# The chunked recurrence of an RWKV block: head products paired across the halves of TensorE, growth and outputs in one PSUM bank, the last growth left out

## The chip, the cores and the metric

One Trainium2 chip, one of its NeuronCores. The metric is the device time of one execution in microseconds (us), lower is better. PE is TensorE, DVE is VectorE, ACT is ScalarE, POOL is GpSimd.

## What is computed

The kernel runs two transformer blocks one after the other over 16 meta tokens and 512 real tokens of width 1024: gated feed-forward layers, a mixer with stick-breaking attention and an RWKV-7 recurrence (first block), three attention branches (second block), and norms. The change touches the RWKV-7 recurrence of the first block alone. For each of 8 heads of width 64, with a state S of 64 x 64:

```python
def step(S, inp):
    r_t, w_t, k_t, v_t, kk_t, a_t = inp
    sa = jnp.einsum('bhij,bhj->bhi', S, -kk_t)
    S = (S * w_t[:, :, None, :] + sa[..., None] * (kk_t * a_t)[:, :, None, :]
         + v_t[..., None] * k_t[:, :, None, :])
    return S, jnp.einsum('bhij,bhj->bhi', S, r_t)
```

The outputs of the 512 real tokens go through a norm over each head, a bonus term and a gate, and then into the output projection.

## The kernel before

The recurrence is computed in nine chunks of 64 tokens (CH); the first holds the meta tokens. Within a chunk the 64 steps become matrix products: scores between the prepared keys and queries, the inverse of a triangular matrix built by doubling, a solve against the incoming state, the growth of the state, and the outputs. Two heads share the 128 partitions: four pairs p, and in each pair one head on partitions 0 to 63 and one on 64 to 127. `heads_in_turn` (L2185) lists for each head its own half `f` and the opposite half `u`. Each product of a head is a 64x64 by 64x64 float32 matmul, which TensorE takes as two records in the profile, on one quadrant of its array: input rows `f` or `u`, output partitions `f` or `u`. A group of eight such products goes to one PSUM bank and is then copied or masked out by one instruction of ACT or DVE.

A chunk c goes through 16 steps k:

- k = 0 (L2209): two scores groups, "nb" and "xc", each 64x128 a head, input and output on half f. DVE masks each (L2368).
- k = 1: the first factors "tus" (L2221), one group onto f and then one onto u; for chunk 0 some identity products (L2231); then three turns (L2240), each of four transposes, of BETA, CHI and VV, whose results ACT copies in halves into BCV (L2338, L2340).
- k = 2: the product of scores and values, "xv" (L2249), onto u; ACT copies it into VH (L2345).
- k = 3, 5, 7, 9, 11: a "half" (L2259), input f, onto u, of TU with a level mask LT that POOL makes (L2420); ACT copies it into PM (L2349).
- k = 4, 6, 8, 10, 12: a "corner" (L2269 onto f, L2271 onto u, head by head in turn); DVE adds it to TU (L2388). The last corner has the u part alone (L2390).
- k = 12, for chunks 2 to 5: a product of the bonus (L2278), one 128x512 matmul; DVE multiplies it (L2396).
- k = 13: "ks", keys by the state (L2285), onto u; DVE adds VH into RS (L2401).
- k = 14: "solve" (L2294), input u, onto f; ACT copies it into SA (L2353).
- k = 15: "update", the growth of the state, in two groups (L2301, L2305) that accumulate in one bank; DVE adds the state (L2404) and scales it to the next one (L2407). For c > 0 the outputs in three groups (L2315) that accumulate in another bank; ACT copies them into Y_R (L2357).

`mixed_order` (L2143) sets the order on every engine: in round r the chunks c with 0 <= r - 4c < 16 take their step k = r - 4c, the oldest chunk first. So up to four chunks are under way, four rounds after one another, and from round 12 to 35 every round holds three or four steps of different chunks. Each step's groups are issued whole, one group after another. What is called a round of four in the tables below is four values of r, from the scores of one chunk to those of the next.

PSUM banks are handed out by `taken_in_turn` (L324): the i-th group of the list `chunk_takes` gets bank i mod 4 (banks 0 to 3) and waits for the release of the group four places before it. Groups that use two banks (first factors and corners) take pairs 4/5 and 6/7 in turn, so that each waits for the release of the one two places before. The engines meet through semaphores only; the order in each engine is the order written out.

After the recurrence the head norm starts on PE when the eighth output copy ("yb") is there and the ninth state ("state"); ACT and DVE also wait for that state. No weight is loaded by the recurrence; the loads for the output projection are issued by SyncE well before.

## Time and profile before

| what | us |
| --- | --- |
| median of 3 runs | 2481.23 |
| lowest and highest | 2478.31, 2481.26 |
| the profiled execution | 2476.59 |
| its span | 2474.6 |
| mean granted TensorE clock | 0.989 |

The time of an execution is a little longer than its span, the stretch that the profiler covers. All rows below are of the profiled execution, and their times count from the start of its span. A row of the windows view has the stretch, its length, the busy time and number of records of PE, PEld (weight loads), DVE, ACT and POOL, then the granted TensorE clock, the DMA engines' busy share and GB/s. In a row of the timeline "x16" is the number of records merged into it, and what stands in brackets is how long the engine had been idle before it and which work ended that. Busy times of PE take in a matmul's latency, so a matmul's 218 ns is longer than the distance to the next one.

### The profile page before, as it was taken

How to read it: one execution, taken by the hardware profiler on the slowest of the kernel's cores; microseconds unless marked ns; L12 is line 12 of the kernel's file. 1: busy time of each engine (PE TensorE's matmuls, PEld its weight loads, DVE VectorE, ACT ScalarE, POOL GpSimd, SP SyncE). 2: the span in 40 equal slices, each digit the busy share in tenths (PEclk: the TensorE clock that was granted, in tenths of full speed). 3: DMA queues.
4: the chain of work that ended last, by engine and by line, in shares of the span. 5: the costliest groups of instructions: out<-in, count | busy, mean ns of one | idle time of the engine just before them, and what ended most of it. 6: DMA issues, size and time to landing. Idle time of an engine off the chain costs nothing.

```text
span 2474.6 us, 48942 instructions
## 1 busy us (share of the span) xinstructions
PE 2421.6 (98%) x20393; PEld 2228.6 (90%) x20393; DVE 1707.5 (69%) x2951; ACT 1080.8 (44%) x1980; POOL 98.3 (4%) x108
## 2 busy tenths in 40 slices
PE   9999999999999999999999999999989999999998
PEld 7999999996887989898999999898877888989896
DVE  6878775646556979688879585243986445879694
ACT  5444343334434535356535243212874224535252
POOL 0000001000320000001000002000000000000001
PEclk9999999999999999999999999999999999999999
DMA  4233232220001332332232233222112333233332
GB/s 152 84 106 103 101 96 90 80 81 12 4 10 46 104 110 96 111 96 77 83 122 94 97 102 97 71 93 85 52 51 77 98 94 102 95 103 103 103 93 70
DMA packets 72378, 213.00 MB, mean 86 GB/s; under 512 B 12796, under 2 KB 20028, under 8 KB 72032
## 3 DMA queue, kind: packets, MB, share of 16 engines
q1 hardware_dynamic: 70496, 209.03, 26.4%
q8 instruction: 162, 2.65, 0.4%
q0 software_dynamic: 480, 0.73, 0.1%
q14 instruction: 56, 0.46, 0.1%
q10 hardware_dynamic: 1184, 0.12, 0.0%
HBM read 207.61 MB, written 2.20 MB: 85 GB/s over the span
## 4 chain that ended last, share of the span: by engine, by line
PE 84%; DVE 8%; ACT 5%; issue 3%; DMA 0%; DVEq 0%; ACTq 0%
PE PS L866 21%; PE PS L1401 20%; PE PS L1358 11%; PE PS L1360 10%; PE PS L1359 10%; DVE WL L951 2%; ACT WH L939 1%; PE PS L2259 1%; PE PS L1709 1%; PE PS L1708 1%; PE PS L1710 1%; DVE P L2913 1%; ACT P L2879 1%; PE PS L1236 1%; PE PS L2209 1%
## 5 line engine op out<-in xcount | busy, mean ns | idle before, releaser
L1358 PE MATMUL PS<-OPH,WH 128*128 128x256 f32 (+1 forms) x2112 | 603.0, 285 | 7.4 <-ACT TMP L1456 2.7
L1360 PE MATMUL PS<-OPH,WL 128*128 128x256 f32 (+1 forms) x2112 | 600.0, 284 | 0.0
L1359 PE MATMUL PS<-OPL,WH 128*128 128x256 f32 (+1 forms) x2112 | 598.1, 283 | 0.0
L939 ACT ACTIVATE WH<-WR 128x1024 fp32r<-128x1024 f32 (+2 forms) x277 | 275.6, 995 | 564.3 <-PE PS L866 272.9
L951 DVE TENSOR_TENSOR WL<-WR,WH 128x1024 fp32r<-128x1024 f32 (+2 forms) x277 | 318.5, 1150 | 190.5 <-ACT WH L939 190.2
L1358 PEld LDWEIGHTS PS<-OPH,WH 128*128 128x128 f32 x2112 | 401.4, 190 | 11.2 <-DVE OPL L1108 3.2
L1359 PEld LDWEIGHTS PS<-OPL,WH 128*128 128x128 f32 x2112 | 401.2, 190 | 1.1 <-issue 0.7
L1360 PEld LDWEIGHTS PS<-OPH,WL 128*128 128x128 f32 x2112 | 400.5, 190 | 0.0
L939 ACT ACTIVATE WH<-SUMS 128x512 fp32r<-128x512 f32 x352 | 211.0, 623 | 231.3 <-DVE SUMS L977 188.8
L951 DVE TENSOR_TENSOR WL<-SUMS,WH 128x512 fp32r<-128x512 f32 x352 | 234.1, 684 | 21.0 <-ACT WH L939 20.5
L866 PE MATMUL PS<-NHI,WH 128*128 128x264 f32 (+2 forms) x976 | 237.9, 309 | 1.0 <-ACT TMP L2633 1.0
L866 PE MATMUL PS<-NLO,WH 128*128 128x264 f32 (+2 forms) x976 | 236.0, 308 | 0.0
L866 PE MATMUL PS<-NHI,WL 128*128 128x264 f32 (+2 forms) x976 | 235.3, 306 | 0.0
L866 PEld LDWEIGHTS PS<-NHI,WH 128*128 128x128 f32 x976 | 157.5, 189 | 12.7 <-issue 1.6
L866 PEld LDWEIGHTS PS<-NLO,WH 128*128 128x128 f32 x976 | 158.6, 189 | 8.8
L866 PEld LDWEIGHTS PS<-NHI,WL 128*128 128x128 f32 x976 | 157.9, 189 | 8.3
L1401 PE MATMUL PS<-HH_A,WH 128*128 128x264 f32 (+1 forms) x572 | 152.4, 321 | 0.0
L1401 PE MATMUL PS<-HL_A,WH 128*128 128x264 f32 (+1 forms) x572 | 152.4, 321 | 0.0
L1401 PE MATMUL PS<-HH_A,WL 128*128 128x264 f32 (+1 forms) x572 | 152.0, 320 | 0.0
L1533 DVE TENSOR_TENSOR T<-PS,RT 128x528 f32<-128x528 f32 (+1 forms) x64 | 44.7, 699 | 148.1 <-PE PS L1401 148.1
L1401 PE MATMUL PS<-HH_B,WH 128*128 128x264 f32 (+1 forms) x476 | 127.1, 321 | 0.0
L1401 PE MATMUL PS<-HL_B,WH 128*128 128x264 f32 (+1 forms) x476 | 126.4, 321 | 0.0
(475 smaller groups left out, 4610.9 us busy)
## 6 DMA issues: line engine op xcount, KB each, us to landing
WR<-in_ffn_up SPq DMA_DIRECT2D x64, 512.0 KB, 3.9
WR<-in_ffn_down SPq DMA_DIRECT2D x64, 512.0 KB, 3.7
WR<-in_ffn_gate SPq DMA_DIRECT2D x56, 512.0 KB, 3.9
WR_MORE<-in_ffn_gate SPq DMA_DIRECT2D x32, 512.0 KB, 4.5
WR_MORE<-in_ffn_up SPq DMA_DIRECT2D x24, 512.0 KB, 4.1
WR<-in_ffn_down SPq DMA_DIRECT2D x32, 384.0 KB, 3.2
WR<-in_w_gate SPq DMA_DIRECT2D x24, 512.0 KB, 3.6
WR<-in_w_out SPq DMA_DIRECT2D x16, 512.0 KB, 3.6
```

The source lines that it names most:

```text
L866: last = e.matmul(bank, left[:, cols], right[:, a:b] if right.shape[1] == L else right, start=(kt == 0 and left is wh and right is hi), st ...
L939: e.activation(split_unit(i)[0][:, 0:w], src, ACT.Copy).then_inc(S["w_hi"], 1)
L951: e.tensor_tensor(lo[:, 0:w], src, hi[:, 0:w].bitcast(F32), ALU.subtract).then_inc(S["w_lo"], 1)
L1236: last = e.matmul(at[:, i:i + 1], data[:, a:a + 128], cst("ones", 128, 1), start=opens, stop=k == DT - 1, skip_group_check=True)
L1358: e.matmul(o, wh[:, at:at + 128], hi, start=k == 0 and s in (1, 2, 5), stop=False, skip_group_check=True)
L1359: e.matmul(o, wh[:, at:at + 128], lo, start=False, stop=False, skip_group_check=True)
L1360: last = e.matmul(o, wl[:, at:at + 128], hi, start=False, stop=k == 3, skip_group_check=True)
L1401: last = e.matmul(bank, left[:, cols], right[:, a:b], start=t == first and left is wh and right is hi, stop=t == end - 1 and left is wl, s ...
L1533: e.tensor_tensor(tcols(t, R), pcols(pair_of["down", f, c, m][0], R), tcols(RT, R), ALU.mult).then_inc(S["d_t"], 1)
L1708: e.matmul(o, NHI[:, kt, a:a + 128], wh[:, c], start=kt == 0, stop=False)
L1709: e.matmul(o, NHI[:, kt, a:a + 128], wl[:, c], start=False, stop=False)
L1710: last = e.matmul(o, NLO[:, kt, a:a + 128], wh[:, c], start=False, stop=kt == DT - 1)
```

## The change

The order of PE in the recurrence is no longer one step after another. The rounds are of four kinds, r mod 4: `with_scores`, `with_state`, `with_solve`, `with_growth`. In each, pairs of groups that use different quadrants are issued head by head in turn:

- the first scores (step 0) of one chunk with the values product of the chunk before, which moves from step 2 to step 4;
- keys by state (step 13) with the first part of the growth (moved from step 15 to 13); halves of steps 9 and 5 with the first two parts of the outputs (moved from step 15 to 13); the two groups of the first factors with each other;
- the solve (step 14) with the second scores, which move from step 0 to step 2;
- the half of step 11 with the second part of the growth, and the half of step 7 with the last part of the outputs (step 15).

The three turns of a chunk are spread over the steps 1 (VV), 2 (BETA) and 3 (CHI). The bonus product moves from step 12 to 11. Growth and outputs share bank 3 for good; all other single groups now take banks 0 to 2 in turn. DVE's growth addition waits for the outputs, and ACT's output copy waits for that addition. The growth of chunk 8, whose state nobody reads, is left out, and the head norm waits for state 8. On ACT and DVE the order within a round stays the oldest chunk first.

The diff, cut to its core:

```diff
+        TURNED_AT = {1: 2, 2: 0, 3: 1}
+        GROWTH_BANK = 3
...
-        chunk_bank = taken_in_turn(chunk_takes, 4)
+        chunk_bank = taken_in_turn(chunk_takes, 3)
...
+            def with_scores(steps):
+                if 12 in steps:
+                    corner(steps[12], 4)
+                if 8 in steps:
+                    corner(steps[8], 2)
+                if 4 in steps:
+                    corner(steps[4], 0)
+                new, old = steps.get(0), steps.get(4)
+                if new is not None:
+                    bank = taken("nb", new)
+                if old is not None:
+                    q.wait_ge("xc", old + 1)
+                    q.wait_ge(*turned_out(old, 2))
+                    values_bank = taken("xv", old)
+                for p, f, u in heads_in_turn:
+                    if new is not None:
+                        scored = scores_product(new, bank, BETA, p, f)
+                    if old is not None:
+                        seen = e.matmul(PS[u, values_bank, 64 * p:64 * p + 64], chunk_homes[old % 4][1][f, p, 0],
+                                        chunk_turned[old % 5][f, 2, p], start=p == 0, stop=True, skip_group_check=True)
...
+            def with_state(steps):
+                late = steps.get(13)
+                if late is not None:
+                    q.wait_ge("state", late)
+                    bank = taken("ks", late)
+                    q.wait_ge("grown", min(late, 1))
+                    q.wait_ge("yb", max(late - 1, 0))
+                    for p, f, u in heads_in_turn:
+                        kept = e.matmul(PS[u, bank, 64 * p:64 * p + 64], KAPPA[f, p, tokens_of(late)],
+                                        ST[f, late % 2, p], start=p == 0, stop=True, skip_group_check=True)
+                        if late < 8:
+                            growth_product(late, 0, p, f)
+                    kept.then_inc(S["ks"], 1)
+                for k, x in (9, 0), (5, 1):
+                    c = steps.get(k)
+                    if c is not None:
+                        bank = half_ready(c, (k - 3) // 2)
+                    for p, f, u in heads_in_turn:
+                        if c is not None:
+                            halved = half_product(c, bank, p, f, u)
+                        if late:
+                            outs_product(late, x, p, f)
+                    if c is not None:
+                        halved.then_inc(S["half"], 1)
...
+            def with_solve(steps):
+                late, new = steps.get(14), steps.get(2)
+                if late is not None:
+                    q.wait_ge("rs", late + 1)
+                    q.wait_ge("tu", tu_at[late, 5])
+                    solve_bank = taken("solve", late)
+                if new is not None:
+                    bank = taken("xc", new)
+                for p, f, u in heads_in_turn:
+                    if late is not None:
+                        solved = e.matmul(PS[f, solve_bank, 64 * p:64 * p + 64], chunk_homes[late % 4][2][u, 1, p],
+                                          RS[u, p], start=p == 0, stop=True, skip_group_check=True)
+                    if new is not None:
+                        scored = scores_product(new, bank, CHI, p, f)
...
+                if 10 in steps:
+                    corner(steps[10], 3)
+                if 6 in steps:
+                    corner(steps[6], 1)
+                if new is not None:
+                    turn(new, 0)
+
+            def with_growth(steps):
+                late = steps.get(15)
+                if late is not None:
+                    q.wait_ge("sa", late + 1)
+                c = steps.get(11)
+                if c is not None:
+                    bank = half_ready(c, 4)
+                for p, f, u in heads_in_turn:
+                    if c is not None:
+                        halved = half_product(c, bank, p, f, u)
+                    if late is not None and late < 8:
+                        grown = growth_product(late, 1, p, f)
...
+                for p, f, u in heads_in_turn:
+                    if c is not None:
+                        halved = half_product(c, bank, p, f, u)
+                    if late:
+                        seen = outs_product(late, 2, p, f)
...
+                    halved.then_inc(S["half"], 1)
+                    turn(c, 1)
...
+            for r in range(4 * 8 + 16):
+                steps = {k: (r - k) // 4 for k in range(r % 4, 16, 4) if 0 <= r - k < 36}
+                (with_scores, with_state, with_solve, with_growth)[r % 4](steps)
...
                     q.wait_ge("outs", c)
-                    e.activation(Y_R[:, :, t0:t0 + CH], four(chunk_bank["outs", c][0]), ACT.Copy).then_inc(S["yb"], 1)
+                    q.wait_ge("grown", min(c + 1, 8))
+                    e.activation(Y_R[:, :, t0:t0 + CH], PS[:, GROWTH_BANK, 256:512].rearrange("p (a n) -> p a n", a=4),
+                                 ACT.Copy).then_inc(S["yb"], 1)
...
-                if k == 15:
+                if k == 15 and c < 8:
                     q.wait_ge("updated", c + 1)
-                    e.tensor_tensor(STT, four(chunk_bank["update", c][0]), ST[:, c % 2], ALU.add).then_inc(S["grown"], 1)
+                    q.wait_ge("outs", c)
+                    e.tensor_tensor(STT, four(GROWTH_BANK), ST[:, c % 2], ALU.add).then_inc(S["grown"], 1)
...
             q.wait_ge("yb", 8)
-            q.wait_ge("state", 9)
+            q.wait_ge("state", 8)
```

## Rows read from the trace of the kernel before

**Rows 1.** The page: each engine's busy time.

```profile
PE 2421.6 (98%) x20393; PEld 2228.6 (90%) x20393; DVE 1707.5 (69%) x2951; ACT 1080.8 (44%) x1980; POOL 98.3 (4%) x108
```

**Rows 2.** The windows view of the recurrence, one row from scores to scores.

```profile
613.98:623.31 9.33, 7.24 (x170) 6.80 (x170) 3.46 (x5) 3.90 (x10) 1.45 (x2) 1.00 0.01 2
623.31:631.69 8.38, 7.38 (x241) 6.87 (x238) 4.72 (x7) 3.80 (x10) 2.87 (x4) 1.00 0.02 4
631.69:641.35 9.66, 8.99 (x321) 8.51 (x318) 6.05 (x10) 4.56 (x12) 4.18 (x6) 1.00 0.02 3
641.35:652.21 10.86, 10.65 (x384) 10.14 (x382) 7.48 (x12) 4.95 (x13) 3.64 (x5) 1.00 0.02 5
652.21:665.32 13.11, 13.05 (x435) 11.77 (x432) 8.15 (x14) 5.25 (x14) 4.36 (x5) 1.00 0.02 5
...
691.30:704.25 12.95, 12.89 (x435) 11.69 (x432) 8.36 (x15) 5.24 (x14) 4.37 (x5) 1.00 0.02 4
704.25:737.71 33.46, 29.13 (x1021) 27.18 (x1016) 15.06 (x29) 8.60 (x24) 7.09 (x9) 1.00 0.02 4
```

**Rows 3.** Timeline of PE: start, length, line, operands, records; chunk 0, then chunk 8.

```profile
615.77 0.75 PE L2221 MATMUL PS<-CHANNELS 64*64 64x64 f32 x26
...
616.83 0.63 PE L2231 MATMUL PS<-CST,CHI 64*64 64x64 f32 x8
617.29 0.63 PE L2231 MATMUL PS<-CST,CHANNELS 64*64 64x64 f32 x8
...
727.09 0.68 PE L2259 MATMUL PS<-TU,SMALL 64*64 64x64 f32 x16 [0.53 <-issue]
...
728.24 0.27 PE L2269 MATMUL PS<-SMALL,TU 64*64 64x64 f32 x1
...
728.72 0.22 PE L2271 MATMUL PS<-TU,SMALL 64*64 64x64 f32 x1
```

**Rows 4.** Timeline of PE: the bonus product, its multiplication (DVE), transposes.

```profile
702.04 1.12 PE L2278 MATMUL PS<-BONUS,CST 128*128 128x512 f32 x2
703.09 0.27 PE L2269 MATMUL PS<-TMP,TU 64*64 64x64 f32 x1
...
703.20 0.69 DVE L2396 TENSOR_TENSOR BONUS<-CHANNELS,PS 128x512 f32<-128x512 f32 x1 [0.62 <-PE PS L2278]
...
707.55 0.62 PE L2240 MATMUL PS<-CST,CHANNELS 128*64 128x128 f32 x4
...
708.98 0.39 PE L2294 MATMUL PS<-TMP,TU 64*64 64x64 f32 x6
```

**Rows 5.** Timeline of ACT and DVE: copies and additions behind groups of PE.

```profile
700.63 0.38 ACT L2357 ACTIVATE Y_R<-PS 128x256 f32<-128x256 f32 x1 [1.78 <-PE PS L2315]
700.93 0.38 ACT L2349 ACTIVATE SMALL<-PS 128x256 f32<-128x256 f32 x1
...
703.86 1.28 DVE L2388 TENSOR_TENSOR TU<-TU,PS 128x512 f32<-128x512 f32 x2
...
727.80 0.38 ACT L2349 ACTIVATE SMALL<-PS 128x256 f32<-128x256 f32 x1 [2.64 <-PE PS L2259]
...
729.00 0.69 DVE L2388 TENSOR_TENSOR TU<-TU,PS 128x512 f32<-128x512 f32 x1 [1.69 <-PE PS L2271]
730.30 0.42 DVE L2404 TENSOR_TENSOR STT<-PS,ST 128x256 f32<-128x256 f32 x1 [0.61 <-PE PS L2305]
```

**Rows 6.** Timeline of PE: the first values product.

```profile
620.99 0.68 PE L2249 MATMUL PS<-BCV,XC 64*64 64x64 f32 x16 [1.61 <-ACT BCV L2340]
```

**Rows 7.** Timeline of PE and ACT: the end of the recurrence.

```profile
732.44 0.51 PE L2271 MATMUL PS<-TU,SMALL 64*64 64x64 f32 x10 [0.48 <-ACT SMALL L2349]
...
734.71 0.38 ACT L2353 ACTIVATE TMP<-PS 128x256 f32<-128x256 f32 x1 [2.32 <-PE PS L2294]
737.28 0.38 ACT L2357 ACTIVATE Y_R<-PS 128x256 f32<-128x256 f32 x1 [2.18 <-PE PS L2315]
```

**Rows 8.** The chain of waits, 714 to 722 us: start, length, what.

```profile
720.35 0.83 issue
```

More of the change, by code:

```diff
@@ new lines, in tokens_of, with taken, half_ready, half_product @@
+            def tokens_of(c):
+                return slice(CH * c, CH * c + CH)
+            def taken(*name):
+                bank, free = chunk_bank[name]
+                q.wait_ge(*free)
+                return bank
+            def half_ready(c, x):
+                q.wait_ge("lt", pm_at[c, x])
+                q.wait_ge("tu", tu_at[c, x])
+                return taken("half", c, x)
+            def half_product(c, bank, p, f, u):
+                TU, LT = chunk_homes[c % 4][2:4]
+                return e.matmul(PS[u, bank, 64 * p:64 * p + 64], LT[f, p], TU[f, 0, p], start=p == 0, stop=True,
+                                skip_group_check=True)
@@ new lines, in turn @@
+            def turn(c, g):
+                bank = taken("tr", c, g)
+                width = 2 * CH if c < 8 else CH
+                for p in range(4):
+                    last = e.transpose(PS[0:width, bank, 128 * p:128 * p + 128],
+                                       (BETA, CHI, VV)[g][:, p, CH * c:CH * c + width], cst("ident"))
+                last.then_inc(S["turned"], 1)
+            def with_scores(steps):
[19 more added lines that the diff above has]
+                if new is not None:
+                    scored.then_inc(S["scored"], 1)
+                if old is not None:
+                    seen.then_inc(S["xv"], 1)
@@ L2252, in pe_rwkv @@
-                if 3 <= k < 13 and k % 2 == 1:
-                    x = (k - 3) // 2
-                    bank, free = chunk_bank["half", c, x]
-                    q.wait_ge("lt", pm_at[c, x])
-                    q.wait_ge("tu", tu_at[c, x])
-                    q.wait_ge(*free)
-                    for p, f, u in heads_in_turn:
-                        last = e.matmul(PS[u, bank, 64 * p:64 * p + 64], LT[f, p], TU[f, 0, p], start=p == 0,
-                                        stop=True, skip_group_check=True)
-                    last.then_inc(S["half"], 1)
@@ L2288, in pe_rwkv @@
-                if k == 14:
-                    bank, free = chunk_bank["solve", c]
-                    q.wait_ge("rs", c + 1)
-                    q.wait_ge("tu", tu_at[c, 5])
-                    q.wait_ge(*free)
-                    for p, f, u in heads_in_turn:
-                        last = e.matmul(PS[f, bank, 64 * p:64 * p + 64], TU[u, 1, p], RS[u, p], start=p == 0,
-                                        stop=True, skip_group_check=True)
-                    last.then_inc(S["solved"], 1)
@@ L2494, in dve_head_norm @@
             q.wait_ge("outs", 8)
[L2495 removed]
+            q.wait_ge("state", 8)
             for k in range(4):
```

259 lines of the change are left out of this document (120 added, 139 removed).

## The prediction, made before the changed kernel ran

> **What bounds the kernel now.** I read the page first: TensorE (PE) is busy for 2421.6 us, 98% of the span [rows 1], so only a change that shortens PE's own order, or a wait in it, can pay. Then the windows view, cut where the scores of a new chunk begin. The recurrence is the stretch from 613.98 to 737.71 us, 123.7 us of 2474.6. Its nine pieces [rows 2] show three regimes. In the first two PE is busy 7.24 of 9.33 us and 7.38 of 8.38: waits count. From the fourth to the eighth PE is covered (12.89 of 12.95 us in the last full round, four rounds nearly alike): work counts. In the last, 33.46 us, it is 29.13 busy, and waits count again. VectorE (DVE) has 8.36 us of work in a full round and ScalarE (ACT) 5.24. The granted clock is 1.00 in every piece, also where PE is least busy, so I give the clock no share.
>
> The timeline then gives PE's prices. A half, a group of eight head products (16 matmul records) on two quadrants, starts at 727.09 and its copy at 727.80, 0.71 us later. A corner of 32 records, which uses both output halves, has its first at 728.24 and its last at 728.72, and its addition starts at 729.00, 0.76 us after its start [rows 3, 5]: twice the records in the same time, some 0.47 us and the latency. So a quadrant, not the issue of instructions, sets the pace, and two groups can share 0.47 us if they lie on different quadrants; this is what the change tries. A scores group takes 0.9 us (two before 615.77, from 613.98); the identity products on one quadrant take 0.46 us for eight records [rows 3]. Twelve transposes take 1.43 us (707.55 to 708.98), 0.48 for four; alone between small tiles, with an entry and an exit of their own each time, I take 0.6 as an estimate [rows 4]. The bonus product costs 1.05 us (702.04 to 703.09) [rows 4].
>
> Other prices [rows 5]: a wide DVE operation takes 0.69, one behind another 0.60 (1.28 for two); a narrow one 0.42; ACT's copy 0.38, but 0.30 from start to start when both are ready (700.63, 700.93), 0.40 for the turned copies. PE follows a finished copy by 0.05 us.
>
> **The parts, and their sum.** PE's work in a full round after the change: three corners 1.41, scores with values in their shadow 0.9; kept/growth, two halves with outputs, first factors, each 0.47 = 1.88, a turn 0.6; solve under the second scores 0.9, two corners 0.94, a turn 0.6; three halves (two carry growth and outputs) 1.41, a turn 0.6, the bonus 1.05. Together 10.3 us, against 12.95 now [rows 2]. Were this all, a full round would win 2.65 us. It isn't: each group now sits between buffers that are released later. With three banks in turn instead of four, I wrote out which release each group waits for. Let u be the start of the half of step 7, which now carries the last outputs.
>
> - Turn of step 3 waits for the copy of half 11. ACT has the output copy ahead of it, which now waits for the outputs (u + 0.71), for the growth addition that itself waits for the outputs (0.42 and 0.04), then 0.30, 0.38 and 0.05: u + 1.9. PE is done at u + 0.94. Wait 0.95.
> - The youngest corner waits for the addition of the oldest one (its pair of banks), which sits behind the bonus multiplication on DVE: the bonus starts 1.16 us after its product (702.04 to 703.20), takes 0.60, the addition 0.42; PE could go 0.25 earlier. Wait 0.25.
> - Half 9 takes the bank of the new scores. DVE masks them after three corner additions and the product's end: u + 6.4 to u + 7.1, PE is there at u + 6.6. Wait 0.5.
> - Half 7 takes the bank of the second scores, whose mask is behind two corner additions on DVE (u + 10.8, 11.4, mask 12.0 to 12.7); PE is there at u + 12.05. Wait 0.65.
>
> Sum of waits 2.35, a round of 12.65, say 12.7. The last three full rounds of before (665.32 to 704.25) are 13.0 each on average [rows 2], so 0.3 each, 0.9; the one before them (13.11) wins 0.4.
>
> First four rounds: now 9.33 + 8.38 + 9.66 + 10.86 = 38.2 [rows 2]. What goes there is the wait of the values product for the turned copies (1.61 us for the first chunk, [rows 6]), as it moves from step 2 to step 4. Round one after: scores 0.9, identity 1.4, first factors 0.47, turn 0.6, scores 0.9, turn 0.6, half 0.47, turn 0.6, 0.45 left of waiting for its copy behind the turned copies, corner 0.47: 6.9. Round two by the same list: 6.9 of work and 0.7 of waits, 7.6. Round three 8.75 and 1.5 (scores' bank, second mask), 10.25; round four 9.25 and 1.5, 10.75. Sum 35.5, so 2.7 less. Note that the third round gets longer than now.
>
> Tail: today the last outputs follow the last solve by growth (0.47 behind ACT's copy) and three output groups, 734.71 to 737.28 [rows 7], 2.57 us. After, two output groups are already done and growth is left out: 0.38 + 0.05 + 0.71 = 1.15, so 1.4 less. In the three rounds before, half 11 no longer waits behind five groups of growth and outputs, but its copy waits for the output copy: half 729.7, outputs 730.2, growth addition 730.9, output copy 731.35, its copy 731.65, corner 732.1 instead of 732.44 [rows 7]: 0.35 each, 1.0. Together 2.4. The last growth's two DVE operations (0.42 each) stand beside output products, hidden by them: nothing. The tail also holds a stall of 0.83 us with no releaser [rows 8]; I count it neither as gone nor as new.
>
> Sum: 2.7 + 0.4 + 0.9 + 2.4 = 6.4, less 0.4 for more such stalls where dense pairs follow each other (bounds: none, and one of 0.83 us in each of the nine rounds, 7 us; I stay near none, since the corners already run at that density and PE is covered for 12.89 of 12.95 us in the full round that holds them [rows 2]). 6.0 us. The profiled execution took 2476.6 us (span 2474.6), so 2470.6 on its scale; it lies 4.6 under the median of the three runs, 2481.2, to which I apply the difference: 2475.2. What follows is PE-bound too (98%) and its weights are loaded already (DMA share 0.02 here), so it should shift whole.
>
> What is costed at nothing: the five level masks on GpSimd (4.37 us a round, [rows 2]) are released by the half before and needed two steps later, some 5 us, so they stay under PE's work; were that cover gone, each half would wait 0.8 us. The sums of scores and values (ACT) move from step 2 to step 4, needed at step 13. The bonus product moves one step ahead, the same work. The second mask moves from step 0 to step 2 and is the fourth wait above. No DMA is issued by the moved steps, and no queue of one is passed. The wait for a ninth state falls away; the head norm waits for the last output copy as now.
>
> The unshown price is that of the pairs: no row has a group of halves with outputs, or a solve beside scores. Lower bound 0.47, that of a corner (same alternation of output halves over one input half); upper bound 0.94, the two in turn. I take 0.47, since the halves and outputs have exactly the corner's pattern.
>
> The Trainium skill, page "TensorEngine Tiling (Array Packing)", section "PSUM Bottleneck", speaks against such a change: tiling makes TensorE quicker, not the copying out of PSUM. By engine totals it would not bind here (DVE 8.4 under PE's 10.3), and a round would be 10.3; by my waits for single copies it is 12.7. No run here shows which yet.
>
> **Rivals.**
> *The copies keep up* (0.06). DVE's total is 8.36, ACT's 5.24 a round; if their queues fit better than I wrote out, the full rounds fall to 10.3 to 11: four times 2.3 more, and some in the fill, 2464. Against: the four waits above follow from queue order.
> *New waits take nearly all* (0.32). Each wait 0.1 to 0.2 us longer than walked, and a full round is 13.0 or over; rounds three and four give back what one and two win. The tail's 2.4 and part of the fill stay: 2478 (-1 to -5).
> *Pairs run one behind the other* (0.12, slower). Alternating onto the other half could stall each product on its neighbour. Six pairs lie on the round's chain (half 7, half 9, half 5, first factors, values, solve), 0.47 each, 2.8 a round: 15.5 for 13.0 in four rounds, +10, while fill and tail keep some 4: 2487. It decides from 0.64 us a pair on (6.0 us over 36 pairs on the chain). Against it stands the corner row. That the kernel's pairs are no pairs at all is in this case.
>
> **How the numbers follow.** My case, 0.50: 5 to 9 us faster, 2472 to 2476. A measurement of this kernel tells 0.2%, 5 us, from no change, and my centre lies just beyond. Faster is 0.50 + 0.06 = 0.56, same 0.32, slower 0.12. Range: down to 2469 for waits that are shorter, up to 2482.5 through the second case and the beginning of the third; runs of one kernel differ by 3 us.
>
> **What would show it.** Windows: nb-to-nb distance about 7, 7.6, 10.3, 10.8, then 12.7 four times, a tail near 31; PE busy under 12 in a full round. Waits: the step 3 turn and half 9 on ACT and DVE, the half of step 7 on the second mask. 32 records of a half/output pair within 0.5 us. Last scores to first centering 31 us instead of 33.5. I am wrong if pairs take 0.9, if full rounds are 11 or less, or if new stalls appear at another place than these four.

## The result, and the profile after

| | before | after |
| --- | --- | --- |
| median, runs side by side (7 and 7) | 2480.28 us | 2488.15 us |
| lowest and highest | 2476.90, 2482.19 | 2485.33, 2491.07 |
| the profiled execution | 2476.59 | 2485.33 |
| its span | 2474.6 | 2483.3 |
| recurrence, first scores to head norm | 123.73 | 132.18 |

The ratio is 1.0034, with a 95% interval from 1.0024 to 1.0043: slower by 7.9 us. The forecast was 6 us faster, 2475.2, with a range up to 2482.5. The recurrence alone took 8.45 us more, so that is where to look; on the page the kernels are otherwise alike:

```profile
PE 2416.2 (97%) x20361; PEld 2216.7 (89%) x20361; DVE 1708.1 (69%) x2949; ACT 1080.1 (43%) x1980; POOL 95.4 (4%) x108
...
q8 instruction: 162, 2.65, 0.4%
```

PE has 5.4 us less busy time than in [rows 1] and 32 of its records fewer (the last growth), and yet the time is longer: what grew is idle time. The last line, a DMA queue that carries instructions (packets, MB, share), will matter below; before has the same one.

The windows view of after, cut at the scores of each chunk as in [rows 2] (stretch, length, busy time and records of PE, PEld, DVE, ACT, POOL, clock, DMA share, GB/s):

```profile
614.51:622.65 8.14, 6.86 (x151) 5.98 (x153) 3.46 (x5) 3.52 (x9) 1.45 (x2) 1.00 0.01 2
622.65:631.48 8.83, 7.91 (x251) 6.75 (x245) 5.04 (x7) 3.80 (x10) 2.90 (x4) 1.00 0.01 4
631.48:642.62 11.14, 9.73 (x329) 8.54 (x324) 6.07 (x9) 4.46 (x12) 3.64 (x5) 1.00 0.01 3
642.62:654.39 11.77, 10.80 (x390) 9.57 (x390) 7.26 (x12) 4.95 (x13) 3.77 (x5) 1.00 0.02 5
654.39:668.85 14.46, 11.72 (x443) 9.76 (x440) 8.52 (x14) 5.13 (x14) 3.63 (x5) 1.00 0.02 5
...
697.48:712.16 14.68, 11.76 (x443) 9.79 (x438) 8.55 (x15) 5.12 (x14) 3.63 (x5) 1.00 0.02 4
712.16:746.69 34.53, 24.97 (x1017) 22.26 (x1007) 14.21 (x27) 8.58 (x25) 7.00 (x9) 0.95 0.02 4
```

Only the first round is shorter, 8.14 for 9.33. A full round takes 14.4 us where before took 13.0 and I had walked 12.7, though PE's busy time fell from 12.9 to 11.8 as meant. Grouped in three, against before and against the walk:

| stretch | before | walked | after |
| --- | --- | --- | --- |
| first four rounds | 38.23 | 35.5 | 39.88 |
| four full rounds | 52.04 | 50.8 | 57.77 |
| the rest | 33.46 | 31.1 | 34.53 |

Next, whether the pairs run as pairs. PE's timeline of after, where the half of step 5 (L2224) runs with the second part of the outputs (L2242), and then the first factors begin (L2333):

```profile
700.67 0.24 PE L2224 MATMUL PS<-TU,TMP 64*64 64x64 f32 x1
700.68 0.27 PE L2242 MATMUL PS<-XC,BCV 64*64 64x64 f32 x1
...
701.16 0.22 PE L2333 MATMUL PS<-CHANNELS 64*64 64x64 f32 x1
```

16 products in 0.48 us, where eight took 0.47 in [rows 3]. The unshown price was right, at its lower bound. The same timeline, those rows of the full round from 692.14 to 706.80 that had an idle stretch before them:

```profile
694.22 0.66 PE L2261 MATMUL PS<-CST,CHI 128*128 128x128 f32 x4 [0.92 <-ACT SMALL L2440]
...
699.44 0.24 PE L2224 MATMUL PS<-TU,SMALL 64*64 64x64 f32 x1 [0.45 <-DVE NB L2461]
...
700.55 0.27 PE L2242 MATMUL PS<-CHANNELS,ST 64*64 64x64 f32 x1 [0.42 <-issue]
...
704.37 0.27 PE L2253 MATMUL PS<-TU,SMALL 64*64 64x64 f32 x1 [0.56 <-issue]
...
706.80 0.24 PE L2224 MATMUL PS<-TU,TMP 64*64 64x64 f32 x1 [0.41 <-DVE XC L2461]
```

Three of the waits that I had written out stand at their places: the turn of step 3 behind ACT's copy, half 9 behind the mask of the new scores, half 7 behind the second mask. The fourth, 0.25 us at the youngest corner, is there too: 0.37 us pass between the last product before it (696.59) and its first (696.96). Its idle time is just too short for a row here; one round later it has one:

```profile
724.84 0.24 PE L2251 MATMUL PS<-SMALL,TU 64*64 64x64 f32 x1 [0.15 <-DVE TU L2483]
```

Between the waits are two stops that nothing released. From start to start they are longer than the idle time in brackets, which counts from the modelled end of the product before: 0.64 us (699.91 to 700.55) and 0.78 (703.58 to 704.37), 1.42 us in this round. The first falls into the middle of a group: 15 of the 16 records of that part of the outputs had gone, and the last came 0.64 us late. No semaphore stands there.

The waits view of PE over the recurrence (line, what it waited for, us, times, longest), after:

```profile
PE PS L2224 <- DVE NB L2461: 3.3, 7, 0.7
PE PS L2261 <- ACT TMP L2440: 2.8, 3, 0.9
PE PS L2224 <- DVE XC L2461: 2.2, 6, 0.5
PE PS L2251 <- ACT SMALL L2440: 1.9, 2, 1.3
PE PS L2261 <- ACT SMALL L2440: 1.8, 2, 0.9
PE PS L2242 <- issue: 1.8, 4, 0.8
PE PS L2253 <- ACT SMALL L2440: 1.6, 1, 1.6
```

All its rows on copies and masks sum to 18.0 us in 29 waits, and those on "issue" to 6.0 us in 12. The same view of before has 4.9 in 7 and 2.2 in 4. From start to start, the four full rounds of after hold seven stops without a releaser, 4.84 us in all, and 10.84 us in 16 waits at the four places; those of before hold no such stop that the view lists.

### The profile page after: what moved, and what is told of

It reads as the page before. It is cut to its first block, busy times and chain, and to the rows that moved or that the text cites. A ratio compares the mean times of both kernels' runs of the same rounds, so it can differ in the third digit from the quotient of the medians.

```text
span 2483.3 us, 48900 instructions
## 1 busy us (share of the span) xinstructions
PE 2416.2 (97%) x20361; PEld 2216.7 (89%) x20361; DVE 1708.1 (69%) x2949; ACT 1080.1 (43%) x1980; POOL 95.4 (4%) x108
## 4 chain that ended last, share of the span: by engine, by line
PE 83%; DVE 8%; ACT 5%; issue 3%; DMA 1%; DVEq 0%; ACTq 0%
PE PS L866 21%; PE PS L1401 20%; PE PS L1358 11%; PE PS L1359 10%; PE PS L1360 10%; DVE WL L951 2%; ACT WH L939 1%; PE PS L1709 1%; PE PS L1708 1%; PE PS L1710 1%; DVE P L3007 1%; ACT P L2973 1%; PE PS L1236 1%; DVE SUMS L977 1%; PE PS L2228 1%
## 5 line engine op out<-in xcount | busy, mean ns | idle before, releaser
L1358 PEld LDWEIGHTS PS<-OPH,WH 128*128 128x128 f32 x2112 | 402.3, 190 | 10.3 <-DVE OPL L1108 2.9
L866 PEld LDWEIGHTS PS<-NHI,WH 128*128 128x128 f32 x976 | 157.3, 189 | 12.7 <-issue 1.6
```

The source lines that it names most:

```text
L866: last = e.matmul(bank, left[:, cols], right[:, a:b] if right.shape[1] == L else right, start=(kt == 0 and left is wh and right is hi), st ...
L1358: e.matmul(o, wh[:, at:at + 128], hi, start=k == 0 and s in (1, 2, 5), stop=False, skip_group_check=True)
```

## The experiments

Two theories. **S, supply:** the stops without a releaser are PE out of instructions. I counted PE's records (loads, products, semaphores) in the two traces: 14 of the 16 stops in the two recurrences stand 256 records apart (give or take one), or a multiple of 256, and each of these ends 2.2 to 3.0 us after a 16 KB packet of the instruction queue has started, at whatever product it then is. The two others (627.76 in after, 727.09 in before) are off this count and stay unexplained. **Q, quadrants and copies:** PE is paced by its quadrants and by the copies and masks alone, and the stops are a few odd delays. A third, **W**, adds to either that the waits that I walked are worth their price.

**1. A dense stretch by itself.** The kernel before with a block of products between recurrence and head norm: 512 products of 64x64 by 64x64 in the order of a corner, then 128 with 256 columns. Nothing waits in it.

```diff
+            for n in range(32):
+                tok = slice(CH * (n % 8), CH * (n % 8) + CH)
+                for p, f, u in heads_in_turn:
+                    e.matmul(PS[f, 4, 64 * p:64 * p + 64], KAPPA[f, p, tok], BETA[f, p, tok], ...)
+                    e.matmul(PS[u, 5, 64 * p:64 * p + 64], BETA[f, p, tok], KAPPA[f, p, tok], ...)
```

> The kernel before, with products between the recurrence and the head norm that nothing reads and nothing holds up: 512 products of 64x64 by 64x64 (2048 records: a weight load and a matmul, twice, for each), in the corner's pattern on four quadrants, then 128 products of 64x64 by 64x256 (512 records). Theory S (PE's instructions come in blocks of 256, and a block takes some 3.5 us however fast the records run): the 2048 records take 8 x 3.5 = 28 us instead of 8 x 1.9 = 15 us, in bursts with a gap at every 256th record; the 512 wide ones take about 14 us, set by the quadrants, without gaps. Rival Q (the quadrants alone set the pace, the gaps of the changed kernel are waits for data that the profile does not name): 15 us and no gaps, 14 us. The whole kernel is 43 or 29 us longer than the one before.

Measured: 2523.24 us in one run, 42.7 over before. Its timeline of PE with the idle stretches, the windows from stop to stop and then of the part with 256 columns, its waits view and the line of the instruction queue:

```profile
750.87 0.21 PE L2448 MATMUL PS<-CHANNELS 64*64 64x64 f32 x1 [1.38 <-issue]
...
754.34 0.21 PE L2448 MATMUL PS<-CHANNELS 64*64 64x64 f32 x1 [1.38 <-issue]
```

```profile
743.65:747.39 3.74, 2.09 (x128) 1.96 (x128) 2.92 (x6) 0.00 (x0) 0.00 (x0) 1.00 0.36 131
...
750.87:754.34 3.47, 2.09 (x130) 1.96 (x129) 0.00 (x0) 0.00 (x0) 0.00 (x0) 1.00 0.02 5
743.65:765.50 21.85, 12.55 (x768) 11.75 (x768) 2.92 (x6) 0.00 (x0) 0.00 (x0) 1.00 0.08 26
...
767.60:783.00 15.40, 15.01 (x255) 12.63 (x246) 0.00 (x0) 0.00 (x0) 0.00 (x0) 1.00 0.01 2
```

```profile
PE PS L2448 <- issue: 11.0, 7, 1.7
```

```profile
q8 instruction: 172, 2.82, 0.5%
```

128 products and 128 loads, 256 records, run in some 1.9 us, then PE stands still until 3.47 to 3.75 us have passed since the last stop ended. Six such blocks, up to the end of the seventh stop at 765.57, take 21.92 us, 3.65 each, or 14.3 ns a record. Seven stops sum to 11.0 us. With 256 columns a product is longer, and PE is busy for 15.01 of 15.40 us. 2560 records more have brought ten packets and 0.17 MB more: 256 records to a packet of 16 KB. Instructions come in such packets while the kernel runs, and in this stretch no block came in less than 3.47 us. S is shown for this stretch and Q, which had 29 us more for the whole kernel, is out.

The trace also shows the rhythm. Each of the packets starts 1.06 to 1.53 us after PE has gone on from the stop before, and PE goes on again 2.2 to 2.7 us after the packet's start. So a block costs a little over 1 us until the next packet starts, and the packet's 2.2 us or more. In the recurrences of all 14 traces the latter holds without exception: PE never enters a block less than 2.16 us after its packet has started.

The Trainium skill, page "Perfetto Trace Analysis", section "The 4-stage abstract model", gives an instruction 64 bytes; 256 of them are 16,384 bytes, one such packet. Its page "Trainium Architecture — The Big Picture", section "The software stack", says that a program's instruction streams are brought to the engines when it is loaded; the 162 packets within one execution speak against reading this as "all of them", and the measurement decides.

**2. Moving the count.** The kernel after, with small products in place of some filler of an earlier stage, to shift all later products by a part of a block. A miss of design: the filler that I changed is called in the first feed-forward too.

```diff
-            for _ in range(times):
+            for _ in range(times - 2):
...
+            for _ in range(34):
+                e.matmul(PS[:, 3, 0:8], FILLER[:, 0:128], FILLER[:, 0:8], start=True, stop=True, skip_group_check=True)
```

> The changed kernel, with two of the 14 opening filler products replaced by 34 narrow ones: some 128 records more ahead of the recurrence, no other work. Theory S: the gaps without a releaser (699.91 and 703.58 in the profile of the changed kernel, each 256 records apart or a multiple of it) sit at other groups, again at multiples of 256 records from one another, shifted by about 128 records; the time stays within 3 us. Rival Q (they are waits for data): the gaps stay at the same groups, the half of step 5 and the corner of step 10.

Measured: 2565.84 us in one run. The shift was of 780 records, three blocks and 12. In the trace 11 of the 12 stops of the recurrence stood again on the same count, so 12 records earlier in their groups. The twelfth, which was off the count in after (627.76), moved with its own product, by 12 records. A small step, not the one meant, but it goes as S said: the stops keep to the count and not to a product. The time says nothing; the products cost what they cost in the feed-forward.

**3. The two orders that my walk named.** The kernel after; in each round ACT takes the output copy behind the copies of the halves, and DVE the second mask ahead of the corner additions. Then each alone.

```diff
+        act_order = sorted(mixed_order, key=lambda ck: (4 * ck[0] + ck[1], ck[1] == 15))
-            for c, k in mixed_order:
+            for c, k in act_order:
...
+        dve_order = sorted(mixed_order, key=lambda ck: (4 * ck[0] + ck[1], ck[1] != 2))
-            for c, k in mixed_order:
+            for c, k in dve_order:
```

> The changed kernel with two queues put in another order, nothing else: ACT makes the output copy (step 15) last in its round, after the copies of the halves, and DVE makes the second mask (step 2) ahead of the corner additions. Theory W (the new waits for released banks make the round long): the waits of the step 3 turn (1.14 us) and of the half of step 7 (0.5 us) go, 1.5 us a full round, 5 full rounds and as many shorter ones: 10 us less than the changed kernel, 2478, under the kernel before. Theory S: the round cannot fall under 3.4 x 3.5 = 12 us whatever the waits, since it has some 900 records; freed stretches run into the next block: 0.5 us a round, 3 to 5 us less, 2484.

> The kernel after with one edit: in each round ScalarE takes the output copy behind the copies of the halves. It takes the first of my four waits away (0.95 us a full round, walked), over some seven rounds. W (my walk, each wait is worth what it is priced at): 4 to 6 us less than after, 2483. S with slack (a wait and a missing block of instructions can overlap): 2 to 4, 2485. If the two order edits together gave 8.3 and do not overlap, this and the next kernel sum to 8.3.

> The kernel after with the other edit: VectorE takes the second mask first in its round, ahead of the corner additions. It takes the fourth wait away (0.65 us a full round, walked). W: 3 to 4 us less than after, 2484.5. S with slack: 1 to 3, 2486.

Measured: both 2479.89 us, ratio to before 1.0002 (0.9992 to 1.0011), 8.3 less than after. The output copy alone 2481.03, 7.1 less; the mask alone 2484.58, 3.6 less. W's figures, 4 to 6 and 3 to 4, were low for the copy and right for the mask, and together they overlap by 2.4; for both at once W had 10. S's, 3 to 5 for both and 2 to 4 and 1 to 3 alone, were all too low: they let a wait and a stop overlap. The three stretches, of the kernel with both, then with the copy alone, in the windows view:

```profile
614.42:654.23 39.81, 35.30 (x1083) 30.67 (x1085) 22.15 (x33) 16.62 (x44) 11.65 (x16) 1.00 0.02 3
654.23:706.50 52.27, 46.40 (x1730) 38.90 (x1729) 33.63 (x56) 20.74 (x56) 15.51 (x20) 1.00 0.02 5
706.50:737.63 31.13, 24.43 (x1016) 21.46 (x1007) 13.94 (x27) 9.00 (x25) 7.00 (x9) 1.00 0.02 4
```

```profile
656.72:709.25 52.53, 46.76 (x1733) 39.10 (x1730) 34.02 (x56) 20.94 (x56) 15.04 (x20) 1.00 0.02 5
709.25:739.86 30.61, 24.26 (x1017) 21.44 (x1008) 13.94 (x27) 9.03 (x25) 7.03 (x9) 1.00 0.02 5
```

Look at the second stretch. Two waits a full round, 1.6 us as walked, are gone, and the four full rounds fall from 57.77 to 52.27: to just what before has, 52.04, and not to the 44.4 that my walk would give without them (four times 12.7 less 1.6). PE still idles 5.9 of these 52.27 us, a part of it before half 9. The stops without a releaser are untouched: seven, 4.66 us from start to start, where after has seven and 4.84. So the waits came off in full, and the stops stayed. The records that I counted in the stretch are 3476, 13.6 blocks, at 3.85 us each. Before's are 3468 in 52.04 us, 3.84 each, some 5% above the probe's 3.65. That the two meet doesn't show one cause: before has no listed stop in its full rounds, and a group alone takes 14.7 ns a record on its quadrants anyway.

**4. Cheaper order in the kernel before.** The two groups of the first factors, one after the other before, are issued as a pair.

```diff
-                    for w in range(2):
-                        for p, f, u in heads_in_turn:
+                    for p, f, u in heads_in_turn:
+                        for w in range(2):
```

> The kernel before with one pair of the change alone: the two groups of the first factors are issued head by head in turn, onto both output halves, without any new wait. PE's work falls by 0.47 us in each of nine chunks, in rounds where PE is covered. Theory W: 4 us less than before, a little under for the first two rounds. Theory S: a full round of before (13.0 us for some 890 records) already lies at 3.7 us for 256 records, so little of it shows: under 1.5 us less.

Measured: 2479.91 us, ratio 0.9995 (0.9986 to 1.0004), not to be told from no change. Full rounds, windows view:

```profile
652.32:704.72 52.40, 51.92 (x1732) 46.76 (x1725) 33.07 (x56) 21.07 (x56) 17.44 (x20) 1.00 0.02 5
```

52.40 for 52.04. But the run doesn't part the theories, since the pair was hardly worth anything: in full rounds the first factors take 0.78 us (0.96 in the first) from their first product to the first transpose, and 0.91 (1.07) before, so 0.11 to 0.13 a round and not 0.47. In before's order the first of the two groups already runs beside the end of the half ahead of it, on other quadrants. The half microsecond won in four rounds went into stops: one of 0.45 us from start to start at 675.31 and one of 0.22, both on the count of 256, where before ran through.

**5. More records, hardly more work.** The kernel before with 16 tiny products (8 columns) a chunk, 64 records, behind the first factors.

```diff
+                    for p, f, u in heads_in_turn:
+                        for w, o in enumerate((f, u)):
+                            last = e.matmul(PS[o, bank + w, 256:264], KAPPA[f, p, tok], BETA[f, p, CH * c:CH * c + 8],
+                                            start=False, stop=True, skip_group_check=True)
```

> The kernel before with 16 products of 64x64 by 64x8 more in step 1 of each chunk, on four quadrants, into unread columns of the first factors' banks: 64 records a chunk, hardly any columns. Theory S (a block of 256 PE instructions takes 3.5 us or more to arrive): 64 records cost 0.9 us in each of the rounds where PE is covered, 5 to 8 us in all, as if they were full products. Rival Q (the quadrants alone set the pace): 32 matmul records on four quadrants at some 25 ns each, 0.2 us a chunk, 2 us in all.

Measured: 2484.44 us, ratio 1.0021 (1.0011 to 1.0031), 4.6 over its own runs of before (2479.88). Nearer to S than to Q, and just under S's band. In the trace the four full rounds took 54.35 us, 2.3 more, for 256 records more: 3.74 us a block, the nearest to the probe's pace of all complete kernels. But it isn't stops that grew: the full rounds list only one, 0.44 us from start to start. The first factors with the tiny products take 1.33 us in most rounds, for 0.91, so the products' own time, 0.42 us a round and twice what Q had, is 1.7 of the 2.3. And the first four rounds grew too, by 1.8. This run speaks for a Q with a dearer product rather than for S.

**6. Fewer records, the same order.** The kernel after without two of the three parts of the outputs for chunks 1 to 7; then the same on the kernel with both orders. These parts lie on the quadrants opposite to the halves of steps 9 and 5 and run in their shadow (the pair above took 0.48 us).

```diff
-                        if late:
+                        if late == 8:
                             outs_product(late, x, p, f)
```

> The kernel after without the first two parts of the outputs (the state and the value part) for chunks 1 to 7: 16 products, 64 records of PE, fewer a chunk; every wait, bank and release stays. Left out of the computation: those two parts, so Y_R of these chunks is incomplete. The 16 products lie on quadrants opposite to those of the halves of steps 9 and 5, one for one. Theory S (PE's instructions arrive in blocks of 256 records, at least 3.5 us apart): 448 records fewer at 8.7 ns (what the padded kernel showed, 5 us for 576) to 14.5 ns (3.7 us over 256) each, 3.9 to 6.5 us less than after, about 2483.5, and fewer stalls without a releaser. Rival Q (quadrants and copies alone set the pace): the products are in the shadow of the halves, 0 to 0.5 us less, 2488. A fall of 2 or less speaks for Q.

> The kernel with both order edits, and without the two output parts of chunks 1 to 7 (64 records a chunk fewer; Y_R of these chunks is incomplete). With two waits gone it should hang on the supply more than after does. S: 4 to 6.5 us less than the kernel with both order edits, 2474 to 2476, faster than before though before does more of these products. Q: 0 to 0.5 less, 2479.5.

Measured: 2480.47 us, 7.7 less than after; and 2472.93, ratio 0.9968 (0.9955 to 0.9981), 7.0 less than with both orders. Q had 0 to 0.5. Windows of the first, and the half of step 9 that has lost its partner:

```profile
618.29:658.13 39.84, 35.52 (x1082) 30.86 (x1084) 21.50 (x33) 16.77 (x44) 12.21 (x16) 1.00 0.01 3
658.13:712.11 53.98, 45.28 (x1602) 38.25 (x1601) 33.51 (x56) 20.53 (x56) 15.84 (x20) 1.00 0.02 4
712.11:743.67 31.56, 23.20 (x921) 20.57 (x911) 14.31 (x27) 8.59 (x25) 6.98 (x9) 1.00 0.02 4
```

```profile
700.95 0.68 PE L2224 MATMUL PS<-TU,SMALL 64*64 64x64 f32 x16 [0.44 <-DVE NB L2461]
701.44 0.49 PE L2224 MATMUL PS<-TU,TMP 64*64 64x64 f32 x10
```

And the one stop without a releaser that the waits view of its four full rounds still lists:

```profile
PE PS L2253 <- issue: 1.1, 1, 1.1
```

The half alone takes 0.49 us from start to the next, as with a partner: on the quadrants the partner had been free. The first four rounds, from which no product was taken, are as in after (39.84 for 39.88). The four full rounds lost 3.8 us with 256 records, 14.8 ns a record, close to the probe's 14.3; over the recurrence the waits on copies hardly changed (17.3 us in 29), those on "issue" fell from 6.0 to 3.0. In the four full rounds the stops fell from 4.84 us in seven to 1.34 in one, from start to start: 3.5 of the 3.8 us. This is the run that shows the supply at work inside the recurrence. Both medians fell by more than S had said. Not all of it is supply: the last stretch fell by 3.0, of which up to 1.7 is a stretch of low clock that after's trace has there and this one hasn't (see below). In the trace of the second, full rounds fell by 2.4 (52.27 to 49.84) and the whole recurrence by 2.5 of the 7.0, under S's 4 and over Q's 0.5; the rest lies outside it, where the same instructions ran somewhat quicker, and I did not find why.

**7. Three parts without pairs.** On the kernel before: the values product at step 4; the end shortened (last growth out, last outputs' first two parts behind the keys by state); and both, with each round's outputs and their copy at its end.

```diff
-                if k == 2:
+                if k == 4:
                     bank, free = chunk_bank["xv", c]
```

```diff
+                    if c == 8:
+                        outs_products(c, (0, 1))
...
-                if k == 15:
+                if k == 15 and c < 8:
...
+                if k == 15 and c > 0:
+                    q.wait_ge("sa", c + 1)
+                    outs_products(c, (0, 1, 2) if c < 8 else (2,)).then_inc(S["outs"], 1)
```

> The kernel before with the values product and its copy moved from step 2 to step 4, unpaired, four banks as before. The prediction priced the waits for turned copies in the first four rounds; no new wait for a released bank is made here. If that term was right: the first two rounds fall by 1.6 and 1.2 us, the third by 0.7, and the whole by 2 to 3 us. If the copies that ACT makes are late for the next group instead (the turned copies stand ahead of the half's copy), less than 1 us is left.

> The kernel before with the end of the change alone: the growth of chunk 8 left out and its first two output groups issued at step 13; one output group follows the last solve. The prediction priced this at 1.4 us (copy of the solve to the last output copy 1.15 us for 2.57 us). Theory S adds nothing here, PE waits for data there: 1.4 us less, under what the runs can tell, to be read in the trace. Rival: the two output groups delay the last solve by their 0.94 us and half of it is given back.

> The kernel before with values at step 4, the short end, and the outputs of every chunk issued at the end of their round, behind the halves, as ACT's output copy is; nothing is paired and four banks are kept. Theory S: in full rounds nothing is gained (some 890 records a round, 13.0 us), in the fill 2 us, at the end 1.4 us and in the three rounds of the tail, where half 11 no longer waits behind three output groups, up to 1 us each: 5 us less than before, 2475. Theory W (new waits for released banks decide): the order of takes is new here too, so some full rounds grow, and 2478 to 2481.

Measured: values at step 4 2479.96 us, ratio 1.0001 (0.9991 to 1.0011); short end 2478.82, 0.9993 (0.9984 to 1.0003), the two not to be told from no change; all three 2477.27, 0.9987 (0.9978 to 0.9996), some 3 us less than before, between S's 2475 and W's 2478 to 2481, and the fastest complete kernel of the study. Windows of the first (first four rounds), of the second (its second round and the last stretch), and of the third:

```profile
618.23:657.09 38.86, 34.10 (x1094) 31.91 (x1094) 21.39 (x34) 16.83 (x44) 12.13 (x16) 1.00 0.01 4
```

```profile
624.18:634.21 10.03, 9.03 (x249) 8.52 (x242) 4.56 (x7) 3.80 (x10) 2.70 (x4) 0.83 0.02 3
...
708.18:739.43 31.25, 27.85 (x1000) 26.18 (x992) 14.38 (x27) 8.60 (x24) 7.09 (x9) 1.00 0.02 4
```

```profile
618.40:656.07 37.67, 33.77 (x1093) 31.71 (x1093) 21.27 (x34) 16.87 (x44) 12.68 (x16) 1.00 0.02 4
656.07:708.94 52.87, 52.24 (x1727) 47.29 (x1725) 33.76 (x56) 21.39 (x56) 17.00 (x20) 1.00 0.02 4
708.94:740.00 31.06, 27.60 (x1003) 26.07 (x998) 14.24 (x27) 9.26 (x25) 7.10 (x9) 1.00 0.02 4
```

The move of the values product wins a microsecond in the first round (its wait of [rows 6] is gone) and gives it back in the third and fourth, where the trace has two stops on the count of 256 (1.42 and 0.38 us from start to start), so the first four rounds stand at 38.86 for 38.23: the gain of 2.7 us that I had put on this stretch isn't in the move itself. The short end wins 2.2 us in the last stretch of its trace, where 1.4 was walked for it; its median moved by 1.1, within the noise. And no complete kernel got its four full rounds below 52 us.

## Why the prediction was wrong

**The price of a pair: right.** 0.48 us for 16 products.

**PE's work in a full round, 10.3 us: nearly right, but not all that bounds.** Without stops and waits, 42.1 of the 57.77 us are left, 10.5 a round. I read 12.89 busy of 12.95 us [rows 2] as PE's quadrants at work, and for before that stands: its blocks take from 2.90 to 5.02 us there, and at their ends no gap from start to start is over 0.16 us. What I didn't see is how near the supply lay: 3.84 us a block on average, against 3.65 in the probe where nothing else bound. A full round has some 869 records, 3.4 blocks, 12.4 us at the probe's pace (an estimate), whatever lies in whose shadow. Pairing halves the time of a group and leaves its instructions. A group alone is 32 records in 0.47 us, 14.7 ns each, which happens to be the pace of supply; a pair is 64 in 0.48, twice that pace. "So a quadrant, not the issue of instructions, sets the pace" was read from a single corner, and holds for one.

**The step that failed** is the last term of the sum, 0.4 us "for more such stalls where dense pairs follow each other", with "bounds: none, and one of 0.83 us in each of the nine rounds, 7 us; I stay near none, since the corners already run at that density". The corners do, but for half a microsecond at a time, with slower groups between them. The walked round of 12.7 holds 2.35 us of waits and then 869 records in the other 10.3, 11.9 ns each, quicker than they come. Over the recurrence the stops without a releaser rose from 3.10 us in four to 8.75 in twelve, start to start, so 5.65 more for the 0.4: nearer to the bound of 7 than to none. In the four full rounds, where before lists none, the walk missed by 7.0 us: 4.8 are these stops, 1.4 longer waits, 0.9 work. Waits and supply add up instead of hiding each other: taking two of the waits out left the stops as they were (run 3), and taking 256 records out of these rounds took 3.5 us of stops away (run 6). The step is the largest, not the only one: from 6.0 us less to 8.45 more are 14.4 us, of which the full rounds are 7.0 and the first four and the last stretch, below, 4.4 and 3.4 (less the 0.4).

**The four waits: right in place and nearly in price.** From start to start they took 1.14, 0.37, 0.66 and on average 0.55 us a full round, 2.7 together, the products' usual distance of some 0.05 each included; I had 0.95, 0.25, 0.5 and 0.65, together 2.35. Without the two that an order can remove, the median falls by 8.3 us, of which the output copy's is 7.1. In the full rounds I had 1.6 us for these two, and 1.4 were won (57.77 to 52.27, by four). The Trainium skill's page "TensorEngine Tiling (Array Packing)", section "PSUM Bottleneck", says that after tiling the copying out of PSUM may become what binds. Here it held in part, by the order of single copies and not by totals: DVE is busy 8.5 and ACT 5.1 of 14.7 us.

**First four rounds, 2.7 us less: wrong, 1.65 more.** In round one I left 0.45 us of waiting for the first half's copy. ACT has the turned copies of two turns ahead of it, and PE waited 1.28:

```profile
622.13 0.27 PE L2251 MATMUL PS<-SMALL,TU 64*64 64x64 f32 x1 [1.28 <-ACT SMALL L2440]
```

The other rounds missed by 1.0 us on average, with waits on the new scores' mask of up to 0.69. Neither order edit changed this stretch (39.81, 39.88), nor did records removed later (39.84). Little of it is supply: after's trace lists two stops without a releaser here, 0.98 us from start to start, of which one (0.43) is on the count of 256, and before's none.

**The rest, 2.4 us less: 1.4 right, 1.0 wrong.** The end is as walked. From ACT's copy of the solve to the head norm it is 745.09 to 746.69, 1.6 us, where before took 3.0 (734.71 in [rows 7] to 737.71). The timelines of ACT and PE:

```profile
742.11 0.38 ACT L2449 ACTIVATE Y_R<-PS 128x256 f32<-128x256 f32 x1 [3.03 <-DVE STT L2498]
742.39 0.38 ACT L2440 ACTIVATE SMALL<-PS 128x256 f32<-128x256 f32 x1
745.09 0.38 ACT L2444 ACTIVATE TMP<-PS 128x256 f32<-128x256 f32 x1 [2.32 <-PE PS L2348]
```

```profile
742.82 0.27 PE L2253 MATMUL PS<-TU,SMALL 64*64 64x64 f32 x2 [1.63 <-ACT SMALL L2440]
...
746.69 0.70 PE L2540 MATMUL PS<-Y_R,CST 128*128 128x512 f32 x1 [0.48 <-ACT Y_R L2449]
```

The three rounds before it were to win 0.35 each. The copy of half 11 (742.39) stands behind the output copy, and that behind DVE's growth addition, and PE waits 1.63 us for a corner that waited 0.48 in [rows 7]. With the output copy last this stretch is 30.61 us, under the 31.1 walked. Some of the 34.53 us is the clock, which I had given no share:

```profile
732.00:736.00 4.00, 2.22 (x85) 2.09 (x85) 1.85 (x4) 0.94 (x3) 0.72 (x1) 0.87 0.01 4
736.00:738.40 2.40, 2.36 (x74) 2.20 (x68) 0.58 (x2) 0.38 (x1) 0.73 (x1) 0.51 0.04 7
```

For some 3.4 us TensorE ran at the lower of its two levels (1.2 GHz), after a stretch in which PE had waited. It costs 1.7 us at most, half of that time, and the last stretch is 3.4 over the walk. Whether the new order invites it is open: the shifted kernel of run 2 shows the same dip at the same instructions (a clock of 0.51 from 815.5 to 818.9 us, and a last stretch of 33.8 us), the five other kernels with that order show none there, and the kernel with the short end shows one (0.83) in its second round, whose instructions are those of before.

**The rivals.** "New waits take nearly all" came nearest, with a full round of 13.0 or over, but ended at 2478. My slower rival, pairs one behind the other, had the sign and the wrong mechanism. That PE's instructions could be what is scarce was in none.

## What to carry to other kernels

Small matrix products are paid twice, in time on the array and in instructions, and the second bill doesn't shrink when products share the array. Before pairing or packing, count PE's records in the stretch and divide by its length: near 14 to 15 ns a record, as here before the change, an order that packs the same products closer ran into stops, and fewer or larger products are what helps. Price each product's own time too: a product of 8 columns was no cheap filler (run 5). And when groups take turns in fewer banks, write out for each engine which copy stands behind which: moving one output copy behind the others was worth 7 us here, as much as the whole change cost.

## What the runs showed of the hardware that was not expected

- PE's instructions arrive during the execution, in 16 KB packets of 256 records. Where nothing else bound, in the probe, a block came every 3.47 to 3.75 us (3.65 over six); in the recurrences of the 14 traces no two packets start less than 3.25 us apart. Products of 64x64 by 64x64 in float32, four records each, use a block up in 1.9 us and then stop; in the part with 256 columns PE was busy for 15.01 of 15.40 us.
- Such a stop can stand within a group of products, has "issue" as its releaser, and so looks like an odd delay. The profile shows it too short: 0.64 us from start to start is 0.42 of idle time, since the modelled durations of the products (218 ns) cover the rest.
- The packets hardly run ahead of PE. In the 14 recurrences each one starts from 1.1 us before to 3.0 us after PE enters the block before its own, by the median of a trace 0.9 to 1.2 after. A wait can push it back: after enters a block at 678.02, waits for ACT's copy until 679.75, and the next packet starts at 680.75 only. That would explain why waits and stops add; no run tests it.
- TensorE's time for a product did not shrink with its columns: 16 products of 64x64 by 64x8 on four quadrants added 0.42 us, where 16 of 64x64 by 64x64 as a pair took 0.48.
- The same first stage began at 613.4 us in one profiled execution and at 618.4 in another, with the same instructions ahead of it. A single trace is therefore compared by stretches, and only medians by their ends.
